# A two-layer gated mixer kernel: the output projection taken in block pairs of seven products

## The reference

```python
h = rms_norm(x, norm_g)
proj = h @ w_in                       # q k v, z_a, p_in, z_b, u, v_sgu, z_c, glu_a, glu_b, z_d, merge
...                                   # four branches o_a .. o_d, each (1024, 512)
branch_out = einsum('bsnw,nwd->bsnd', branches, w_branch)     # 4 x (1024, 1024)
gates = sigmoid(merge.reshape(B, S, 4, D))
mixed = sum(gates * branch_out, axis=2)
return x + mixed @ w_out              # w_out is 1024 x 1024
```

## Time and profile before

| | us |
|---|---|
| median of 3 runs (2089.29 to 2090.38) | 2089.48 |
| the profiled execution | 2089.1 |
| its span, first to last instruction | 2087.3 |
| TensorE busy | 2073.3 (99%) |
| GpSimd busy | 1232.5 (59%) |
| VectorE busy | 1266.3 (61%) |
| ScalarE busy | 844.7 (40%) |

### The profile page before, as it was taken

The page is one execution under the profiler, slowest core; times in us unless marked ns, Lnnn a source line. Parts: engine busy times, 40 slices in busy tenths (PEclk is TensorE's granted clock), DMA queues, the critical chain, the costliest instruction groups (busy, mean ns, idle before and its releaser), DMA issues.

```text
span 2087.3 us, 27166 instructions
## 1 busy us (share of the span) xinstructions
PE 2073.3 (99%) x9760; PEld 1715.9 (82%) x9760; DVE 1266.3 (61%) x1529; ACT 844.7 (40%) x1617; POOL 1232.5 (59%) x940
## 2 busy tenths in 40 slices
PE   9999999999999999999999999999999999999999
PEld 8788877888888888888888888778888888888887
DVE  5896544688878635335357864447888785452331
ACT  6634544333233334425445245533432343353331
POOL 2356444776769767554423564447766786676543
PEclk9999999999999999999999999999999999999999
DMA  7112231313431343415431032223134313433153
GB/s 273 46 36 96 91 102 64 124 53 79 86 79 54 81 81 73 139 51 181 152 93 46 31 101 97 91 97 101 51 81 94 68 52 81 91 66 141 52 201 101
DMA packets 112469, 192.02 MB, mean 92 GB/s; under 512 B 14032, under 2 KB 23504, under 8 KB 112336
## 3 DMA queue, kind: packets, MB, share of 16 engines
q1 hardware_dynamic: 94304, 159.53, 24.2%
q0 software_dynamic: 9216, 16.78, 6.0%
q10 hardware_dynamic: 8816, 13.97, 1.8%
HBM read 148.28 MB, written 41.95 MB: 91 GB/s over the span
## 4 chain that ended last, share of the span: by engine, by line
PE 93%; POOL 2%; DVE 2%; DMA 1%; ACT 1%; issue 0%; SPq 0%; DVEq 0%; POOLq 0%; ACTq 0%
PE acc L678 80%; PE aux L741 5%; PE acc L741 3%; POOL wlo L609 1%; PE aux L813 1%; PE aux L832 1%; PE aux L823 1%; POOL wsum L613 1%; PE aux L847 1%; DMA x<-x 1%; DVE x L1423 0%; PE aux L775 0%; PE acc L775 0%; PE aux L789 0%; PE aux L854 0%
## 5 line engine op out<-in xcount | busy, mean ns | idle before, releaser
L609 POOL TENSOR_TENSOR wlo<-raw,whi 128x512 fp32r<-128x512 f32 x424 | 582.7, 1375 | 583.4 <-ACT whi L936 582.3
L678 PE MATMUL acc<-fhi,whi 128*128 128x512 f32 x2048 | 801.6, 391 | 3.7 <-DVE oc L1413 2.4
L678 PE MATMUL acc<-fhi,wlo 128*128 128x512 f32 x2048 | 797.2, 389 | 0.0
L678 PE MATMUL acc<-flo,whi 128*128 128x512 f32 x2048 | 797.0, 389 | 0.0
L678 PEld LDWEIGHTS acc<-fhi,whi 128*128 128x128 f32 x2048 | 384.4, 188 | 86.3 <-issue 6.1
L678 PEld LDWEIGHTS acc<-fhi,wlo 128*128 128x128 f32 x2048 | 384.4, 188 | 80.4
L678 PEld LDWEIGHTS acc<-flo,whi 128*128 128x128 f32 x2048 | 384.5, 188 | 78.3
L936 ACT ACTIVATE whi<-raw 128x512 fp32r<-128x512 f32 x424 | 265.7, 627 | 452.5 <-PE acc L678 390.3
L609 POOL TENSOR_TENSOR wlo<-wsum,whi 128x512 fp32r<-128x512 f32 x192 | 273.3, 1423 | 176.7 <-ACT whi L936 176.2
L1423 DVE SCALAR_TENSOR_TENSOR aux<-conv,allp,aux 128x1024 f32<-128x1024 f32 x232 | 299.1, 1289 | 20.0 <-issue 0.4
L678 PE MATMUL acc<-bhi,whi 128*128 128x512 f32 x512 | 201.7, 394 | 0.0
(11 more groups left out here) (194 smaller groups left out, 2298.7 us busy)
## 6 DMA issues: line engine op xcount, KB each, us to landing
raw<-wstream SPq DMA_DIRECT2D x424, 256.0 KB, 2.7
md<-prev POOLq DMA_DIRECT2D x64, 256.0 KB, 4.2
x<-x SPq DMA_DIRECT2D x32, 256.0 KB, 5.2
md<-prev SPq DMA_DIRECT2D x32, 256.0 KB, 3.5
out<-x ACTq DMA_DIRECT2D x32, 256.0 KB, 2.2
mx<-md SPq DMA_DIRECT2D x24, 256.0 KB, 4.9
xrow<-x_rows SPq DMA_DIRECT2D x8, 512.0 KB, 6.7
qd<-qst ACTq DMA_DIRECT2D x16, 256.0 KB, 2.2
```

Of the source, the lines that this page charges most:

```text
L609: nc.gpsimd.tensor_tensor(wlo[:, f % SLOTS, :], src, whi[:, f % SLOTS, :].bitcast(F32), ALU.subtract).then_inc(lo_made, 1)
L678: mm = nc.tensor.matmul(dst, w, m[:, kt0 + k, cols], start=first and k == 0 and n == 0, stop=last and k == UK - 1 and n == 2, skip_group_c ...
```

## The change

The output projection becomes a stage "O" of four pairs. The first pair is done plainly with four weight units in the order w11, w21, w12, w22, each for both token halves (8 steps), with banks b, a, d, c; the other three use the seven products. So 8 + 3 x 7 = 29 steps stand where 32 stood, and 16 weight units where 32 were loaded. The merged blocks of B11, B12, B21, B22 are rounded into the slots that MD3's products p1, p4, p2, p3 leave, and the four differences F5, F7, F6, F4 are formed in place on VectorE (`mix_form`) and rounded into the slots that p5, p7, p6 and the plain pair's w21 leave. So there are 32 roundings and 32 low parts in place of 16, and 16 formed blocks. The x blocks are finished in another order (`X_DONE`), and the second layer's VS takes them in pairs k, t = 1, 0. The token sums of the second layer move from the middle of k = 0 into k = 1, and the last tile of k = 0 to the end of k = 1. In the first layer SyncE's wait for the norms, with the two transfers behind it, moves behind all x tiles. `last_mixes` moves to the end of U's first pair. The diff, cut, its indentation shortened:

```diff
-  ("ZD", 2), ("MD", 4))
+  ("ZD", 2), ("MD", 4), ("O", 4))
...
+FIRST_OUT = ("w11", "w21", "w12", "w22")
+FIRST_BANK = {(0, 0): "b", (0, 1): "a", (1, 0): "d", (1, 1): "c"}
...
+MIX_HI = [("B11", d) for d in range(4)] + [("F5", d) for d in range(4)]
+MIX_HI += [("B21", 0), ("B21", 1), ("B22", 0), ("B22", 1)] + [("B12", d) for d in range(4)]
+MIX_HI += [("B21", 2), ("B21", 3), ("B22", 2), ("B22", 3)]
+MIX_HI += [(q, d) for q in ("F7", "F6", "F4") for d in range(4)]
+MIX_REST = MIX_HI
+MIX_FORMS = [(q, d) for q in ("F5", "F7", "F6", "F4") for d in range(4)]
...
-        if k == 5:
-            sp.wait_ge(norms_stored, 16)
-            sp.dma_start(spreads[:], rd[0:1].rearrange("o t p -> o (t p)").partition_broadcast(P)
-                         ).then_inc(spread_loaded, 16)
-            sp.dma_start(rms[:], rd[0].rearrange("t p -> p t"), allow_slow_non_contiguous=True
-                         ).then_inc(rms_turned, 16)
+    sp.wait_ge(norms_stored, 16)
+    sp.dma_start(spreads[:], rd[0:1].rearrange("o t p -> o (t p)").partition_broadcast(P)
+                 ).then_inc(spread_loaded, 16)
+    sp.dma_start(rms[:], rd[0].rearrange("t p -> p t"), allow_slow_non_contiguous=True
+                 ).then_inc(rms_turned, 16)
...
+        load_pair(L, "O", 0)
+        sp.wait_ge(step_done, stepped(L, "MD", 3, "B22"))
+        src = x if L == 0 else out
+        if L:
+            for p in range(2):
+                sp.wait_ge(x_stored[p], 16 * KT * L)
+        for i in range(4):
+            if i:
+                load_pair(L, "O", i)
+            for k in ((0, 1), (2, 3), (4, 5), (6, 7))[i]:
+                for p in range(2):
+                    sp.dma_start(x_block(k, p), src[k * P:(k + 1) * P, p * HALF:(p + 1) * HALF]
+                                 ).then_inc(xin_loaded[k], 16)
...
+            if (st, i) == ("O", 1) and q in ("p6", "p5", "p7", "p4"):
+                pe.wait_ge(mix_ready, mix_n(L, {"p6": "F6", "p5": "F5", "p7": "F7", "p4": "F4"}[q], 3))
...
+            work = [(k, tile) for tile in (4, 5, 6, 7, 0, 1, 2, 3)]
+            if name == "VS" and L and k < 2:
+                work = work[:7] + ([(0, 3), (1, 3)] if k else [])
+            for n_tile, (kx, tile) in enumerate(work):
                 if name == "VS" and n_tile == 4:
                     pe.wait_ge(x_ready, x_turn(L, k, 0) + 1)
-                if name == "VS" and L and k == 0:
-                    if n_tile >= 4:
-                        pe.wait_ge(taken["abcd"[tile]], L * BANK_N["abcd"[tile]])
-                    if n_tile == 6:
+                if name == "VS" and L and k == 0 and n_tile >= 4:
+                    pe.wait_ge(taken["abcd"[tile]], L * BANK_N["abcd"[tile]])
+                if name == "VS" and L and k == 1:
+                    if n_tile == 2:
...
+    def first_out(L):
+        for q in FIRST_OUT:
+            half, tile = {"w11": (0, 0), "w21": (0, 1), "w12": (1, 0), "w22": (1, 1)}[q]
+            pe.wait_ge(lo_made, split(L, "O", 0, q))
+            slot = (L * FORMS + FORM["O", 0, q]) % SLOTS
+            for t in range(2):
+                operand = ("B11", "B12") if half == 0 else ("B21", "B22")
+                if tile == 0:
+                    pe.wait_ge(mix_ready, mix_n(L, operand[t], 3))
+                bank = FIRST_BANK[tile, t]
+                if half == 0:
+                    pe.wait_ge(taken[bank], bank_n(L, bank, ("O", 0)))
+                s = MIX_SLOT[operand[t]]
+                three(BANK_AP[bank], fhi[s], flo[s], slot, 0, half == 0, half == 1).then_inc(step_done, 1)
...
+    def mix_rounded(L, q, ds):
+        if q == "F4":
+            act.wait_ge(step_done, stepped(L, "O", 0, "w21", 1))
+        else:
+            act.wait_ge(step_done, stepped(L, "MD", 3, SLOT_LEFT[q]))
+        for e in ds:
+            d, t = mix_src(q, e)
+            if q[0] == "F":
+                act.wait_ge(mix_formed, L * len(MIX_FORMS) + MIX_FORMS.index((q, e)) + 1)
+            else:
+                b = {(0, 0): "B11", (0, 1): "B12", (1, 1): "B22", (1, 0): "B21"}[d % 2, t]
+                bank = BANK_OF[b]
+                act.wait_ge(taken[bank], bank_n(L, bank, ("MD", d // 2), 2 if b == "B11" else 3))
+            copy(fhi[MIX_SLOT[q]][:, e, :], merged_block(d, t)).then_inc(mix_hi, 1)
...
+        merge_pair(L, "MD", 3, {"p1": lambda: mixes(("B11", range(4))),
+                                "p7": lambda: mixes(("F5", range(4))),
+                                "p3": lambda: mixes(("B21", (0, 1)), ("B22", (0, 1))),
+                                "p4": lambda: mixes(("B12", range(4))),
+                                "bA": lambda: mixes(("B21", (2, 3)), ("B22", (2,)))})
...
+        mixes(("B22", (3,)), ("F7", range(4)))
+        next_high(L, "O", 0, "w11")
+        mixes(("F6", range(4)))
+        next_high(L, "O", 0, "w21")
+        mixes(("F4", range(4)))
+        new_x(0)
+        next_high(L, "O", 0, "w12")
+        new_x(1)
+        new_x(2)
+        next_high(L, "O", 0, "w22")
+        new_x(3)
...
+        for i in range(1, 4):
+            begin_pair(L, "O", i, {"p6": lambda i=i: next_rounded(i, "p6", (0, 1)),
+                                   "p5": lambda i=i: next_rounded(i, "p6", (2, 3))})
+            next_high(L, "O", i, "p7")
+            new_x(4 * i)
+            next_high(L, "O", i, "p2")
+            new_x(4 * i + 1)
+            next_rounded(i, "p2", (4,))
+            next_high(L, "O", i, "p3")
+            new_x(4 * i + 2)
+            next_rounded(i, "p2", (5,))
+            next_high(L, "O", i, "p4")
+            new_x(4 * i + 3)
+        next_rounded(3, "p2", (6, 7))
...
-                last_mixes()
-                dve.drain()
             mul(b_[:, HALF:SEQ], b_[:, HALF:SEQ], BANK_AP["b"]).then_inc(taken["b"], 1)
...
+            if i == 0:
+                last_mixes()
+            else:
...
+        def mix_rest(q, ds):
+            for e in ds:
+                dve.wait_ge(mix_hi, mix_n(L, q, e))
+                dve.drain()
+                s = MIX_SLOT[q]
+                sub(flo[s][:, e, :], merged_block(*mix_src(q, e)), fhi[s][:, e, :].bitcast(F32)
+                    ).then_inc(mix_ready, 1)
+        def mix_form(q, ds):
+            for e in ds:
+                dve.drain()
+                dst = merged_block(*mix_src(q, e))
+                if q == "F5":
+                    op = sub(dst, dst, merged_block(e, 1))
+                elif q == "F7":
+                    op = sub(dst, merged_block(e + 4, 1), dst)
+                elif q == "F6":
+                    op = scaled(dst, dst, -1.0, merged_block(e, 0), ALU.subtract)
+                else:
+                    op = scaled(dst, merged_block(e + 4, 1), -1.0, dst, ALU.subtract)
+                op.then_inc(mix_formed, 1)
...
+        all4, low2, high2 = range(4), (0, 1), (2, 3)
+        merge_sums(L, "MD", 3, (lambda: mix_rest("B11", all4), lambda: mix_form("F5", low2),
+                                lambda: (mix_form("F5", high2), mix_rest("F5", all4)), nothing,
+                                lambda: (mix_rest("B21", low2), mix_rest("B22", low2)),
+                                lambda: mix_rest("B12", low2), lambda: mix_rest("B12", high2),
+                                lambda: mix_form("F7", low2)))
+        mix_rest("B21", high2)
+        mix_rest("B22", high2)
+        mix_form("F7", high2)
+        mix_form("F6", all4)
+        mix_rest("F7", all4)
+        mix_rest("F6", all4)
+        def squares_behind(n):
+            if L + 1 < LAYERS and n >= 0:
+                square_added(n)
+        def first_x(n):
+            d, t = X_DONE[n]
+            bank = FIRST_BANK[d, t]
+            dve.wait_ge(xin_loaded[d], 32 * (L + 1))
+            dve.wait_ge(step_done, stepped(L, "O", 0, ("w12", "w22")[d], t))
+            add(x_block(d, t), x_block(d, t), BANK_AP[bank]).then_inc(taken[bank], 1)
+            squares_behind(n - 2)
+        first_x(0)
+        mix_form("F4", low2)
+        first_x(1)
+        mix_form("F4", high2)
+        first_x(2)
+        mix_rest("F4", low2)
+        first_x(3)
+        mix_rest("F4", high2)
...
+        def next_rest(i, *ks):
+            if L + 1 < LAYERS and i == 3:
+                for k in ks:
+                    x_rest(L + 1, k, 1)
+                    x_rest(L + 1, k, 0)
...
+            sum_x(L, "O", i)
+            squares_behind(4 * i - 2)
+            sum_v(L, "O", i)
+            squares_behind(4 * i - 1)
+            next_rest(i, 0)
+            sum_22(L, "O", i, BANK_AP["b"])
+            dve.drain()
+            add(x_block(2 * i + 1, 1), x_block(2 * i + 1, 1), BANK_AP["b"]).then_inc(taken["b"], 1)
+            next_rest(i, 1)
+            dve.wait_ge(step_done, stepped(L, "O", i, "p2"))
+            add(x_block(2 * i, 0), x_block(2 * i, 0), BANK_AP["a"]).then_inc(taken["a"], 1)
+            squares_behind(4 * i)
+            next_rest(i, 2)
+            sum_12(L, "O", i, BANK_AP["c"])
+            dve.drain()
```

(81 more changed lines are left out.)

140 lines of the change are left out of this document (37 added, 103 removed).

## The result

The kernel before took 2089.87 us (median of 6 runs, 2089.29 to 2091.26), the changed one 2099.03 us (median of 6, 2095.21 to 2099.66). The ratio is 1.0041, 95% interval 1.0028 to 1.0054: **slower by 9.2 us** (0.4%), where 3.4 us faster was forecast. The profiled execution of the changed kernel took 2099.66 us, its span is 2097.5, the granted clock 0.995 on average.

The account below looks back on a forecast made before the run. TensorE, busy 2073.3 of 2087.3 us, was taken as the bound. Terms -16.3 - 5.2 - 2.4 + 14.0 + 3.0 + 0.8 + 2.7 = -3.4 us gave 2086.0 us, range 2067 to 2096, likeliest case 2081 to 2092.

Parts of the forecast that it names:

- matmuls removed: Output projection: 32 steps become 29 in each layer, 36 matmuls fewer at 0.2267 us each; -16.3 us for two layers.
- first layer's start: Ahead of Q: norms read at about 28, h begins at 36.5, most of TensorE's 4.67 us wait and low clock go; -5.2 us.
- gating mix: U's last mixes: VectorE's two operations move behind the products that free U's banks, removing a 1.22 us wait per layer; -2.4 us.
- VectorE late in the hand-over: MD3 to projection: 11 GpSimd meetings at 0.92 us make TensorE wait 7.0 us per layer, mostly before O1 p1; +14.0 us.
- lower clock behind it: After the roughly 5 us idle time ahead of O1 p1, TensorE's clock falls; +3.0 us for both layers.
- second pair's p5 (ScalarE): O1, first layer: ScalarE rounds p5 only behind F4 and the first x block, which follow VectorE's chain; +0.8 us.
- second layer's start: Ahead of Q: norms stored some 4.6 us later behind a rounding awaiting the end of k = 1, h too; +2.7 us.
- VS of the first layer starts later: ScalarE's 15.1 us of work in the first layer's last pair was taken to fit 19.0 us; costed at nothing.
- The U waits: TensorE's two waits of 1.2 us for VectorE's products in U, forecast to go wholly with the moved mix; -2.4 us.
- The pace holds: Rival: VectorE's hand-over chain takes no longer than 46 us, so 17.8 us of cost do not come; 2068.2 us, chance 0.12.
- VectorE is later still: Rival: each hand-over meeting blocks VectorE for GpSimd's whole 1.3 us, 6.8 us more per layer; 2099.6 us, chance 0.13.
- The norms path costs more: Rival: second layer's h comes 7 us later and the clock falls behind it; +4, 2090 us, chance 0.08 within 2088 to 2093.

Follow-up runs that it names:

- Experiment 1: Changed kernel with GpSimd's weight low parts and sums of the hand-over made on 16 of 512 columns; 2076.67 us, ratio 0.9936 to the kernel before.
- Experiment 4: Changed kernel with SyncE's first-layer wait for the norms and its two transfers put back behind the x tiles of k = 5; 2100.55 us, ratio 1.0053.
- Experiment 3: Changed kernel with ScalarE storing the second layer's norms before its next weight rounding; 2096.44 us, ratio 1.0033 to the kernel before.
- experiment 5: Changed kernel with the gating mix put back ahead of U's products; 2103.47 us, ratio 1.0063 to the kernel before.
- experiment 7: Changed kernel with ScalarE emptying the VS banks ahead of two roundings of h in each layer; 2088.49 us, ratio 0.9993 to the kernel before.
- experiment 10: Changed kernel with GpSimd's low parts of weights in the hand-over cut into halves of 256 columns; 2092.89 us, ratio 1.0015 to the kernel before.
- experiment 2: Changed kernel with 20 unused matmuls added ahead of O1 p1 in both layers, keeping TensorE busy; 2095.41 us, ratio 1.0027 to the kernel before.
- experiment 6: Changed kernel with VectorE's hand-over chain reordered, all four first additions to x ahead of the low parts of F7 and F4; 2099.21 us, ratio 1.0044.
- experiment 8: Changed kernel with reordered hand-over chain, VS banks emptied first, and next layer's norms ahead of the last x low parts and stored first; 2087.27 us, ratio 0.9988.
- experiment 11: Changed kernel with VS banks emptied first and two plain output pairs (30 steps per layer); 2079.04 us, ratio 0.9948 to the kernel before.
- experiment 12: Changed kernel with VS banks emptied first, two plain output pairs and GpSimd's hand-over low parts in halves of 256 columns; 2074.20 us, ratio 0.9925.
- experiment 9: Kernel before, its 32-step projection kept, with the gating mix moved and the VS banks emptied first; 2082.68 us, ratio 0.9965.

## Why the prediction was wrong

The mechanism that the forecast turned on was right, and its sum came out on the wrong side because four terms were off in one direction: the second layer's start by 4.7 us, the first layer's by 4.3, the lower clock by 2.6 and VectorE's lateness by 2.1. Measured from the gaps between TensorE's starts:

| term | predicted | measured |
|---|---|---|
| matmuls removed | -16.3 | -16.3 |
| first layer's start | -5.2 | -0.9 |
| gating mix | -2.4 | -2.8 |
| VectorE late in the hand-over | +14.0 | +16.1 |
| lower clock behind it | +3.0 | +5.6 |
| second pair's p5 (ScalarE) | +0.8 | 0 |
| second layer's start | +2.7 | +7.4 |
| VS of the first layer starts later | 0 | +0.4 |
| sum | -3.4 | +9.5 |

The spans differ by 10.2, and the 0.7 that the table lacks lies in single gaps of under 0.2 us. The profiled executions differ by 10.6, the medians by 9.2. (With a sum of -3.4 the forecast should have read 2086.1, not 2086.0.)

**Right.** *The hand-over.* VectorE was forecast 7.0 us late per layer, in three places of 0.5, 1.6 and 5: the trace has 0.8, 1.7 and 5.1, which with the restarts is 8.0. Eleven meetings of 0.92, 10.1 us, were forecast; the rows hold 10.2. The 57 operations from 935.65 to 989.73 take 54.1 us; without the meetings and 0.7 of waits for ScalarE that is 0.757 each, where 0.74 was taken, and this makes 0.9 us of the difference per layer. Experiment 1 shortened GpSimd's operations and changed nothing else, and the waits went. *The U waits* went, with 1.4 us each from start to start where 1.2 was priced.

The Trainium skill ("SBUF — State Buffer", section "Who interferes with whom") has a VectorE instruction with two SBUF inputs contend with a GpSimd one that reads SBUF. The traces agree: the blocked rows have both inputs in SBUF, and cutting GpSimd's operation cut the delay from 0.92 to 0.39 us. GpSimd pays too: its row at 971.15, in such a meeting, took 1.56 us against the 1.30 of the row at 960.01 in the earlier trace rows, beside an operation that reads PSUM.

**The step that failed: the first layer's start,** where I took -5.2 and had put the other bound at 0, "if the stored norms come later behind the x tiles by as much as was won". That is nearly what happened. I had the norms read at about 28; they were asked for at 31.11. The stretch in which the norms are stored, in the kernel before (us, busy of each engine, PEclk, DMA share, GB/s):

```profile
26.00:28.00 2.00, 2.00 (x11) 1.65 (x10) 1.41 (x2) 2.00 (x4) 0.33 (x1) 1.00 0.09 23
```

and in the changed one, with the store's own row (KB, us to landing):

```profile
26.00:28.00 2.00, 2.00 (x11) 1.65 (x10) 0.91 (x2) 1.66 (x3) 0.00 (x0) 1.00 1.05 385
```

```profile
rd<-rms ACTq DMA_DIRECT2D x1, 4.0 KB, 5.2
```

Before, SyncE's wait left the queues nearly empty, 23 GB/s, and the store landed in 2.3 us. Now the x tiles and weights asked for ahead of it keep them at 385 GB/s: the store, issued at 25.94, lands in 5.2 us. `sgt`, the last input that VectorE waits for ahead of h, is asked for only at 33.06 and takes 6.5 us, so h began at 39.93 against 40.55, and not at 36.5:

```profile
39.63 0.27 DVE L1847 MEMSET sgt<- 64x256 f32 x1 [2.80 <-DMA sgt<-sgu_wt]
39.93 2.08 DVE L1492 SCALAR_TENSOR_TENSOR x<-x,allp,spreads 128x512 f32<-128x512 f32 x3
```

I had taken the landing time of an idle spell that the change itself removes: 2.3 where it was 5.2. Experiment 4 puts the wait back, and with 33 GB/s in the same stretch the store lands in 2.4 us; it prices the whole move at 1.5 us.

The Trainium skill ("DMA: Bandwidth & Descriptors", section "Latency and other measured facts") says that HBM's access time, the larger part of a transfer's fixed cost, grows under load. The trace agrees in direction, 2.3 and 5.2 us for the same 4 KB, but does not show that this is what grew: the store's first packet moved 0.8 us after its issue before and 3.7 us after it now, which is nearly the whole difference, and from the last packet to the landing it was about 0.6 us in both.

**The second layer's start was mis-sized, by more:** 2.7 forecast, 7.4 measured: 5.0 idle ahead of Q, 1.5 for 8 matmuls at the lower clock behind it, 0.9 at the token sums. h began 29.3 us after the layer's start where 22.3 + 4.6 was forecast: 1.0 of the 2.4 us by the store's issue (1062.9, 13.1 after the start, for 12.1), the rest by its landing, 11.2 us where it had taken 9.5. The rounding that I named held the store; a second holder, VectorE's reciprocal behind eight low parts of x (1056.51 to 1061.81), I did not look for. Experiment 3 shows it: with the rounding out of the way the store moved by 1.4 us only, 0.6 of which the whole layer came earlier. Why the landing grew stays open. It is not the row transfers ahead of it on ScalarE's queue: the last of them, issued at 1056.69, landed at 1062.3, before the store was issued. Nor can it be set beside the first layer's store, for this one goes out in 1024 pieces of 4 bytes and that one in 128 pieces of 32. And I counted no lower clock there, though the earlier trace rows show it behind a 4.67 us wait.

**The lower clock** was priced at 1.5 us per wait from the earlier trace rows. In the profile of the changed kernel it was 2.8 us behind O1 p1, but the same wait in the profiles of experiments 3, 4, 5, 7 and 10 has 7 to 12 slow matmuls, 1.5 to 2.5 us, or 3.2 to 4.8 for both layers, and experiment 2, which removed it, won 3.6 us: for an ordinary execution the forecast 3.0 was a little low, and the table's 5.6 belongs to one profile.

**Rivals.** "The pace holds" is refuted by the waits, "VectorE is later still" by the 0.92; that its 2099.6 us is next to the measured 2099.0 is luck, since other terms make up the time. "The norms path costs more" came true (h 7.0 us later than before, counted from the layer's start, and the clock down behind it), together with the forecast rather than instead of it: I had kept apart as cases what adds up.

## What to carry to other kernels

Work saved on the engine that bounds is won only as far as its feeders keep their due times: here 72 matmuls saved cost 5.8 us, while saving 24 matmuls fewer (30 steps per layer in place of 29), which moves the deadline of the formed blocks by one pair, won 9.4 us over that. Count, for the stretch in question, every VectorE operation with both inputs in SBUF against GpSimd's operations, and if they must meet, cut GpSimd's short. A wait whose cause is an overfull chain comes back at the next step when the order alone is changed; one whose cause is a queue order (the banks emptied behind roundings that nobody needed yet) went but for 1.4 of 11.9 us.

## What the runs showed of the hardware

- A VectorE operation with two SBUF inputs that meets a 512-column GpSimd operation loses 0.92 us (0.8 to 1.1), with a 256-column one 0.39 us (0.2 to 0.4); operations with one input in PSUM lose nothing (0.68 to 0.69 us in either case).
- After every wait of TensorE of 3.3 to 5.4 us the clock fell to the 1.2 GHz level (matmuls 0.43 us apart) for 6 to 14 matmuls, at once or up to 1.6 us later, and how many did not follow the length of the wait: 7 behind 4.8 us and 13 behind 4.2 us in the same profile (experiment 10). Of the shorter ones, one of 1.9 us (experiment 3) had 8 behind it too, others of 1.7 and 2.9 us none.
- The clock also fell behind the token sums (a wait of 0.7, then 16 one-column matmuls in 1.9 us) for some 8 matmuls, 1.6 us, in the profiles of experiments 2 to 8 and 10 to 12; it did not in those of the changed kernel and experiment 1, with the same wait and sums, nor in the kernel before and experiment 9, which have the sums without the wait. What decides between the first two groups stays open.
- The same 4 KB store to DRAM, 128 pieces of 32 bytes, landed in 2.3 us with the transfers at 23 GB/s and in 5.2 us at 385 GB/s. A store of as many bytes in 1024 pieces of 4 took 9.5 us in the kernel before and 11.2 in the changed one; its packets in the changed kernel, of which 1024 carry the data:

```profile
q10 hardware_dynamic: 1040, 0.00, 4.1%
```
